# Two transformer blocks on one core: the in-pairs of the state-space tiles move one place, next to the out-pairs

## What is computed

```python
def second_block(x, ...):
    h = rmsnorm(x, norm1_g)
    proj = h @ w_in                       # 2048 -> 2*1024 + 1024 + 3*1024 + 3*2048
    y_a = gmlp_mixer(uv, ...)             # gated mixing in chunks of 128 positions
    y_b = s5_mixer(s5_in, ...)            # the state-space branch
    y_c = stick_breaking_attention(q, k, v)   # 8 heads of 128
    merged = sum over n of sigmoid(gate_n) * (y_n @ w_branch[n])
    x = x + merged @ w_out
    x = x + square(relu(rmsnorm(x) @ w_mlp_in)) @ w_mlp_out
    return rmsnorm(x, final_g)

def s5_mixer(xin, ...):
    u = xin.reshape(bsz, seq, 64 groups, 16 channels)
    bu = einsum('blgh,gph->blgp', u, bb)  # complex, 64 states a group
    s = associative_scan of  s_t = a * s_{t-1} + bu_t   (complex, along the 256 positions)
    y = real(einsum('blgp,ghp->blgh', s, c)) + d * xin
    g = gelu(y)
    return g * sigmoid(g @ w_glu + b_glu)
```

## Time and profile before

| What | Value |
|---|---|
| Time, median of 3 runs | 3231.97 us (3231.28 to 3232.05) |
| Profiled execution, span from first to last instruction | 3233.1 us |
| Profiled execution against the median of the runs | 1.1 us more |
| Mean granted TensorE clock over the span | 0.987 |
| TensorE busy | 3112.4 us, 96% |
| VectorE busy | 1952.8 us, 60% |
| ScalarE busy | 1386.5 us, 43% |
| GpSimd busy | 458.1 us, 14% |
| Chain of waits, share of TensorE and of VectorE | 87% and 7% |

### The profile page before, as it was taken

The page is one execution under the profiler, slowest core; times in us unless marked ns, Lnnn a source line. Parts: engine busy times, 40 slices in busy tenths (PEclk is TensorE's granted clock), DMA queues, the critical chain, the costliest instruction groups (busy, mean ns, idle before and its releaser), DMA issues.

```text
span 3233.1 us, 37776 instructions
## 1 busy us (share of the span) xinstructions
PE 3112.4 (96%) x13864; PEld 2524.0 (78%) x13864; DVE 1952.8 (60%) x2093; ACT 1386.5 (43%) x1613; POOL 458.1 (14%) x423
## 2 busy tenths in 40 slices
PE   6999999999899999999799999999998999999997
PEld 4777788888788888887676667888887888888886
DVE  3566655555777665665568775555555566656665
ACT  4444544444444444444343445444444444444443
POOL 2000101100688000000026550000000000000000
PEclk9999999999999999999899999999999999999999
DMA  5544666656566666665655445666655566666663
GB/s 159 163 139 139 198 206 192 194 175 215 183 214 208 218 188 189 189 188 177 180 163 158 143 133 163 206 215 200 201 195 165 181 190 188 188 188 190 192 188 130
DMA packets 300343, 589.39 MB, mean 182 GB/s; under 512 B 20840, under 2 KB 20944, under 8 KB 298832
## 3 DMA queue, kind: packets, MB, share of 16 engines
q1 hardware_dynamic: 291840, 562.11, 56.4%
q0 software_dynamic: 5760, 24.72, 2.4%
q10 hardware_dynamic: 2640, 1.18, 0.2%
HBM read 575.35 MB, written 12.58 MB: 182 GB/s over the span
## 4 chain that ended last, share of the span: by engine, by line
PE 87%; DVE 7%; ACT 2%; issue 2%; DMA 2%; ACTq 0%; POOL 0%; DVEq 0%; POOLq 0%
PE banks L1354 85%; DVE wlo L868 3%; PE banks L1357 2%; DMA raw<-in_w_in 1%; ACT whi L509 1%; DVE W L894 1%; ACT W L509 1%; DVE W L1270 0%; DMA x<-W 0%; ACTq L825 0%; DMA Z<-in_gm_w_s 0%; ACT L509 0%; DMA raw<-in_w_branch 0%; DVE W L1195 0%; DVE W L1200 0%
## 5 line engine op out<-in xcount | busy, mean ns | idle before, releaser
L868 DVE TENSOR_TENSOR wlo<-raw,whi 128x1024 fp32r<-128x1024 f32 x1048 | 1361.3, 1307 | 1028.8 <-ACT whi L509 1022.4
L509 ACT ACTIVATE whi<-raw 128x1024 fp32r<-128x1024 f32 x1048 | 1100.2, 1059 | 1258.4 <-PE banks L1354 1179.1
L1354 PE MATMUL banks<-whi,XH 128*128 128x512 f32 x2816 | 1125.8, 400 | 35.0 <-DVE wlo L868 30.5
L1354 PE MATMUL banks<-whi,XL 128*128 128x512 f32 x2816 | 1104.5, 392 | 0.0
L1354 PE MATMUL banks<-wlo,XH 128*128 128x512 f32 x2816 | 1104.4, 392 | 0.0
L1354 PE MATMUL banks<-whi,Y 128*128 128x512 f32 x2752 | 863.0, 391 | 10.8 <-DVE Y L879 8.0
L1354 PEld LDWEIGHTS banks<-whi,XH 128*128 128x128 f32 x2816 | 533.5, 189 | 173.7 <-DVE wlo L868 34.8
L1354 PEld LDWEIGHTS banks<-whi,XL 128*128 128x128 f32 x2816 | 532.8, 189 | 114.2
L1354 PEld LDWEIGHTS banks<-wlo,XH 128*128 128x128 f32 x2816 | 534.1, 190 | 105.7
L1354 PEld LDWEIGHTS banks<-whi,Y 128*128 128x128 f32 x2752 | 518.8, 189 | 120.5 <-DVE Y L879 8.4
L1354 PE MATMUL banks<-wlo,Y 128*128 128x512 f32 x1376 | 537.2, 390 | 0.0
(11 more groups left out here) (234 smaller groups left out, 1224.4 us busy)
## 6 DMA issues: line engine op xcount, KB each, us to landing
raw<-in_w_in SPq DMA_DIRECT2D x384, 512.0 KB, 3.9
raw<-in_w_mlp_up SPq DMA_DIRECT2D x128, 512.0 KB, 3.8
raw<-in_w_mlp_down SPq DMA_DIRECT2D x128, 512.0 KB, 3.8
raw<-in_w_mlp_in SPq DMA_DIRECT2D x128, 512.0 KB, 3.8
raw<-in_w_mlp_out SPq DMA_DIRECT2D x128, 512.0 KB, 3.8
raw<-in_w_branch SPq DMA_DIRECT2D x80, 512.0 KB, 4.2
raw<-in_w_out SPq DMA_DIRECT2D x64, 512.0 KB, 4.5
tables<-G POOLq DMA_DIRECT2D x8, 1024.0 KB, 7.8
```

The source lines that it names most:

```text
L509: return nc.scalar.activation(out_, in_, f, **kw)
L868: tt(wlo[:, i % RING, :], raw[:, i % RING, :], whi[:, i % RING, :].bitcast(F32), ALU.subtract)\
L1354: return nc.tensor.matmul(out_, l, r, start=start, stop=stop, **kw)
```

## The change

The in-pair of tile j is issued one place later, behind unit 27+2j instead of unit 26+2j. The out-pairs stay, so that in-pair j stands directly ahead of out-pair j-3. VectorE's, GpSimd's, ScalarE's and SP's programs are the same as before.

```diff
             def s5_in():
                 for j in range(32):
-                    yield S5Q + 2 * j
+                    yield S5Q + 2 * j + 1
                     i, c = j // 4, 32 * (j % 4)
                     if j == 0:
                         pe.wait_ge(S("s5_mT_copied"), 8)
```

## The result

The changed kernel takes **3374.69 us** (median of 4 runs, 3370.96 to 3378.22) against 3232.01 us for the kernel before in the same session (3231.28 to 3232.88). The ratio is 1.0445, 95% interval 1.043 to 1.046: 142.7 us slower. The forecast was 3356 us in a range of 3305 to 3392. The profiled execution took 3378.22 us, with a span of 3376.4 us and a mean granted clock of 0.971. That is 3.5 us above the median, and 143.3 us of span above the profiled execution of before.

What follows compares the result with a forecast made beforehand. The prediction took TensorE to set the pace, with VectorE not far behind. It added 94 us for the lengthened stage and 30 us for the lower clock, 124 us, to the median of 3231.97: 3356 us, range 3305 to 3392.

Steps and rivals of the forecast that it cites:

- Step 1: TensorE's in-pair and out-pair side by side save one seam, 0.2 us at each of 29 shared places, 6 us.
- Step 2: VectorE's tile and split get one out-pair and one unit as cover; loop period 8.8 us if nothing disturbs VectorE.
- Step 3: GpSimd now starts inside VectorE's tile; overlap costs 2.9 us a tile, period 11.5 us, bounds 8.8 and 11.8.
- Step 4: State-space stage summed without the clock, with 28 periods of 11.5 us and two long skip waits: +94 us.
- Step 5: TensorE's idle gaps lower its granted clock: +30 us, bounds nothing and 53 us.
- the forecast's case: VectorE's loop, overlap with GpSimd and a clock that is often low: 3356 us, chance 0.58.
- the clock falls at every tile: Rival: same loop, with the unit behind every tile's gap at half speed: 3379 us, chance 0.12.
- VectorE keeps up, only seams are left: Rival: VectorE's tile and split end before the covering unit does, leaving only the seam saving: 3226 us, chance 0.03.

Runs made afterwards that it cites:

- group at the early place: Kernel before with out-pairs one place earlier (32+2j), beside the unmoved in-pairs, and the skip operations at place 40+8i: 3221.23 us, ratio 0.9966.
- out-pairs moved on: Changed kernel with out-pairs, and the skip operations with them, one place later, so that pairs stand alone again: 3252.16 us, ratio 1.0062.
- the third state buffer: Changed kernel with three state buffers on GpSimd instead of two, and four table buffers instead of five: 3259.75 us, ratio 1.0078.
- the run with filler: Changed kernel with 14 (8 where attention products stand) extra 512-column matmuls, results unused, on TensorE behind units 28+2j: 3342.92 us, ratio 1.0339.
- the run with the out-pair first: Changed kernel with the out-pair issued ahead of the in-pair at their shared place: 3332.7 us, ratio 1.0305.
- the two rearrangements with one more unit of cover and the early skip: Kernel before with out-pairs at 32+2j, 3221.23 us; changed kernel with VectorE's tile at 29+2j, 3222.05 us; both with skip operations at 40+8i.
- the late tile: Changed kernel with VectorE's tile one place later as well, at 29+2j, two units behind its in-pair: 3233.01 us, ratio 1.0005.

## Why the prediction was right, and where its terms were off

**Step 1, seams.** Priced at 0.2 us a place and hidden in the changed kernel; measured 0.27, with no new seam between the pairs. It is indeed hidden behind the wait, and it shows as soon as the wait is gone (group at the early place).

**Step 2, the loop through VectorE.** Right. With out-pairs moved on the period is 8.8 us, the lower bound given.

**Step 3, the overlap.** The mechanism was right, and it is what makes the loss large: the third state buffer takes 115 us away. The term was mis-sized by a detail. The block of VectorE's four operations, GpSimd's four and one split was taken as 6.16 us; in the tile above it runs from 1757.01 to 1763.17 (the unit's start less 0.15), 6.16 us again, so the length held. But I let it begin where GpSimd starts, 2.3 us behind the in-pair, and it begins where L1194 does, 2.52 us behind. Split and unit come at 8.83 instead of 8.6, and the period without the clock is 11.8, the upper bound named in that step, not 11.5. For the 26 regular periods (the 28 from the fourth on, without the two that wait for the skip) that is 7 us: 307.5 in the run with filler, 300.3 predicted with the transposes.

**Step 4, the sum.** The first three periods took 28.5 us (26.8 predicted). The gaps in them of 1.76 to 1.79 us, on which the prediction put no price, were followed once by a mean clock of 0.62 (10.9 us where 9.2 was predicted). The two long waits on the skip are 7.1 us each and their periods 17.9 and 18.5 us; predicted with their share of the clock were 18.9 each, so 1.4 us too much in all.

**Step 5, the clock.** This is where most of the 18.7 us between forecast and median come from. Of the 30 us, 24.5 were for regular periods. There the changed kernel takes 345.8 us and the run with filler 307.5: 38.3 us. The step named nine gaps that attention products shorten and put 0.5 us on each. Eight of them were 2.4 us long, but behind six of the eight the clock was as low as behind the long ones (0.57 at 1941.82). The price of 1.3 us for each of 17 long gaps was low too: 1.6. So the true course lay between the forecast's case and the rival "the clock falls at every tile" (3379). That the rival's number lies nearer to the measured one than the forecast does is in part luck: it has the same loop, 7 us too short, and a price on all 31 gaps. The Trainium skill, page "TensorE: Matmul & The Clock Gate", section "HAM oscillation — how this bites in real kernels", tells of a kernel whose every tile restarts cold behind a wait of some 3 to 5 us. The trace agrees for the 18 regular gaps of 3.1 to 3.8 us, all followed by the lower clock; the eight of 2.4 us are shorter than the page's, and six of them were followed by it too.

The step's premise, that every gap of 2.9 us is followed by the lower clock, held in the trace of before and not everywhere: in the run with the out-pair first, four gaps of 2.88 to 2.90 us were not.

In one line: predicted for in-pair to in-pair over 31 periods 389.9 us with clock, measured 410.7. Of the 21 us, 14 are the clock in regular periods, 7 the block's start and 2 the first periods, less 1.4 at the long waits. It is 21 here and 18.7 against the median mostly because the stage began 2.8 us earlier than in the execution of before.

**The port rule.** The Trainium skill, page "SBUF — State Buffer", section "Who interferes with whom", has it that a VectorE operation with two SBUF inputs and a GpSimd operation that reads SBUF keep each other out, by an exclusive lock. It was the reason to take the 6.16 us over to the new place, and the traces agree: VectorE's four operations stretched to 5.0 us here, and L1191 and L1192, which read PSUM, stayed at 0.69 and 0.68 us beside GpSimd's first two products (run with the out-pair first, 1777.51 and 1778.12).

**The other rivals.** "VectorE keeps up, only seams are left" (3226) did not come about in this kernel, but its saving is what the two rearrangements with one more unit of cover and the early skip gave, with the waits on the skip on top, at 3221 and 3222. Its condition, tile and split done before the covering unit ends, was the right test.

**What the changed profile was to show** was there: tile to tile 11 to 13 us (13.3 at most places, a little over), 3 us of idle time ahead of units 29+2j, GpSimd 2.3 us behind the in-pair (2.32), two waits of 7.1 us on L1207. L1195 and the scans were to be at 1.1 to 1.7 us, and are at 1.51, 1.09 and 1.14.

## What to carry to other kernels

When a step is moved to share a place with another, ask first what its consumer then has as cover: here one unit of 2.95 us less turned an overlap that costs nothing with that unit (the late tile) into 115 us, the clock's share included. The same grouping at the earlier place, or with the consumer moved along, was a gain of 0.3% once the skip was moved as well; with the late tile alone it was none. What a group saves is its seam, 0.27 us, and what it can lose is the whole slack of the engine behind it. And count a recurring TensorE gap as more than its own length: here those of 3.1 to 3.8 us were all followed by the lower clock, at some 1.6 us each.

## What was not expected of the hardware

- TensorE's gaps of 1.8 to 2.9 us were followed by the lower clock in some cases and not in others. In the changed kernel it was the first of three gaps of 1.8 us (0.62 behind it, period 10.9; the two others 8.8) and six of eight of 2.4 us in regular periods (0.57 at 1941.82), while behind the two of 2.39 us the clock stayed at 1.00. With the out-pair first it was ten of 14 of 2.9 us. The three gaps of 1.8 us stand at the same places of the program in five kernels, and the lower clock followed one of them in the changed kernel, two with out-pairs moved on and with filler, and all three with the third buffer and with the out-pair first. So length alone does not decide. No run was made to tell what does, and that stays open.
- Here the two engines that shut each other out corrected themselves. In the run with the group early, a VectorE that comes late lets GpSimd's first product run beside its PSUM operations, and the tile falls from 6.3 to about 5.2 us. This may be why VectorE, busy 96% of the stage, was no bound; no run separates it from the two units of cover.
- An in-pair that uses the array by rows and an out-pair that uses it by columns follow each other at 1.05 us, like a pair and a unit; the turn costs nothing that shows (1700.14 to 1701.19 in the run with the group early).
